# Two of a chunk's four weight sums made by an adding DMA instead of VectorE, in a macaron block with Strassen-Winograd up projections

## The reference

```
def _swiglu(h, w_in, w_out):
    gate, up = jnp.split(h @ w_in, 2, axis=-1)
    return (jax.nn.silu(gate) * up) @ w_out
...
        x = x + FFN_RES * gt1[:, None, :] * _swiglu(h, ffn1_w_in[l], ffn1_w_out[l])
```

## Time and profile before

| | us |
|---|---|
| median of 3 runs | 2106.72 |
| lowest, highest | 2099.39, 2107.37 |
| span of the profiled execution | 2101.5 |

### The profile page before, as it was taken

The page is one execution under the profiler, slowest core; times in us unless marked ns, Lnnn a source line. Parts: engine busy times, 40 slices in busy tenths (PEclk is TensorE's granted clock), DMA queues, the critical chain, the costliest instruction groups (busy, mean ns, idle before and its releaser), DMA issues.

```text
span 2101.5 us, 27713 instructions
## 1 busy us (share of the span) xinstructions
PE 2045.3 (97%) x9921; PEld 1707.3 (81%) x9921; DVE 1370.3 (65%) x1935; ACT 850.6 (40%) x1223; POOL 122.7 (6%) x211
## 2 busy tenths in 40 slices
PE   4999999999999999999999998999999999999998
PEld 4888888888888888888888887887888888888887
DVE  5987777765674567667577578649666666633434
ACT  5432333332343366456456466325333333322322
POOL 6000000001211000000000000000000000001010
PEclk7999999999999999999999999999999999999999
DMA  9344544425865420100111001323233223235453
GB/s 363 98 130 131 142 136 122 120 82 204 301 216 188 130 67 21 40 23 22 32 31 33 19 22 61 100 81 101 80 90 90 70 80 90 85 130 190 163 196 117
DMA packets 185790, 230.87 MB, mean 110 GB/s; under 512 B 7540, under 2 KB 137708, under 8 KB 184940
## 3 DMA queue, kind: packets, MB, share of 16 engines
q1 hardware_dynamic: 155300, 132.72, 20.8%
q0 software_dynamic: 23424, 84.16, 12.0%
q10 hardware_dynamic: 6984, 12.86, 1.8%
HBM read 189.59 MB, written 40.11 MB: 109 GB/s over the span
## 4 chain that ended last, share of the span: by engine, by line
PE 86%; DVE 7%; ACT 3%; DMA 2%; issue 2%; SPq 0%; POOL 0%; DVEq 0%; ACTq 0%
PE ps L728 26%; PE ps L730 25%; PE ps L729 25%; PE ps L997 2%; PE ps L942 1%; PE ps L928 1%; DMA ada_second<-in_w_ada_dram 1%; PE ps L931 1%; PE ps L959 1%; PE ps L958 1%; DMA x_rows<-in_x_dram 1%; PE ps L736 1%; PE ps L744 0%; DMA w_raw<-in_ffn_w_out_dram 0%; PE ps L989 0%
## 5 line engine op out<-in xcount | busy, mean ns | idle before, releaser
L728 PE MATMUL ps<-h_hi,w_hi 128*128 128x512 f32 x720 | 292.9, 407 | 9.1 <-DVE h_lo L1763 5.6
L730 PE MATMUL ps<-h_hi,w_lo 128*128 128x512 f32 x720 | 285.6, 397 | 0.0
L729 PE MATMUL ps<-h_lo,w_hi 128*128 128x512 f32 x720 | 285.1, 396 | 0.0
L728 PE MATMUL ps<-da_hi,dw_hi 128*128 128x512 f32 x704 | 275.6, 391 | 1.3 <-DVE dw_lo L1867 0.9
L730 PE MATMUL ps<-da_hi,dw_lo 128*128 128x512 f32 x704 | 274.1, 389 | 0.0
L729 PE MATMUL ps<-da_lo,dw_hi 128*128 128x512 f32 x704 | 274.0, 389 | 0.0
L728 PE MATMUL ps<-T_hi,op_hi 128*128 128x512 f32 x640 | 249.4, 390 | 0.0
L730 PE MATMUL ps<-T_hi,op_lo 128*128 128x512 f32 x640 | 249.0, 389 | 0.0
L729 PE MATMUL ps<-T_lo,op_hi 128*128 128x512 f32 x640 | 249.0, 389 | 0.0
L1229 ACT ACTIVATE op_hi<-S_f 128x512 fp32r<-128x512 f32 x160 | 100.8, 632 | 309.6 <-PE ps L730 300.4
L1864 DVE TENSOR_TENSOR da_lo<-act_raw,da_hi 128x512 fp32r<-128x512 f32 x88 | 60.9, 692 | 217.9 <-ACT da_hi L1278 217.8
(11 more groups left out here) (286 smaller groups left out, 3513.3 us busy)
## 6 DMA issues: line engine op xcount, KB each, us to landing
w_raw<-in_ffn_w_out_dram POOLq DMA_DIRECT2D x84, 512.0 KB, 3.8
raw<-in_ffn_w_in_dram SPq DMA_DIRECT2D x44, 512.0 KB, 5.3
raw_odd<-in_ffn_w_in_dram SPq DMA_DIRECT2D x44, 512.0 KB, 5.7
act_rows<-act_out SPq DMA_DIRECT2D x44, 512.0 KB, 3.4
act_raw<-act_rows SPq DMA_DIRECT2D x88, 256.0 KB, 2.6
ada_ring<-in_w_ada_dram POOLq DMA_DIRECT2D x32, 512.0 KB, 3.8
raw<-in_w_in_mix_dram SPq DMA_DIRECT2D x29, 512.0 KB, 3.9
ada_late<-in_w_ada_dram POOLq DMA_DIRECT2D x24, 512.0 KB, 4.9
```

Source lines behind the costliest of these rows:

```text
L728: pe.matmul(dst, whi, mhi, start=start, stop=False)
L729: pe.matmul(dst, whi, mlo, start=False, stop=False)
L730: return pe.matmul(dst, wlo, mhi, start=False, stop=stop)
```

## The change

Of the four sums, S0 = a21 + a22 and S2 = a11 + a21 are now made by DMAs. POOL loads one quadrant into the slot from w_in, waits, and adds the other with a DMA whose accumulate operation is an addition. To make both of these additions (S2 was a11 - a21), the lower weight row of the seven products is negated, so the sums S1 and S3, still DVE's, and four reads of products change sign where needed. POOL's new function has two plain DMAs, a wait, and two adding DMAs; for the first Strassen chunk it waits for all T sums, for others until op_lo 6 of the chunk before is written. DVE's `weight_sums` now waits for all four DMAs at its head. POOL's modulation loads of each chunk come behind its sums, and POOL now has an up phase in the second FFN too, between its work for the mixer and the w_out loads. The counter of the silu of c is merged with s_cols.

```diff
-        SUM_AT = {"P5": (0, 1), "P7": (2, 2), "P6": (1, 3), "P3": (3, 4)}
+        SUM_AT = {"P5": (0, 0), "P7": (2, 0), "P6": (1, 1), "P3": (3, 2)}
...
-            def up_body(b, kind, v, k0):
-                if kind & ADDS:
-                    for k in range(k0, k0 + KH):
-                        load_ada(v, k)
-            bodies(pool, ffn1, up_body)
+            def load_sums(f, c):
+
+                if isinstance(c, int) and c == CL:
+                    pool.wait_ge(s_T, (f.i + 1) * T_ALL)
+                else:
+                    pool.wait_ge(s_lo, f.op(c, 6) - Ffn.PRODUCTS)
+                as_k = lambda n: S_f[:, n].rearrange("p (k j) -> p k j", j=P)
+                quad = lambda s, k0: f.w_in[:, k0:k0 + KH, s, c, :]
+                pool.dma_start(as_k(0), quad(1, 0)).then_inc(s_SL, 16)
+                pool.dma_start(as_k(2), quad(0, 0)).then_inc(s_SL, 16)
+                pool.wait_ge(s_SL, f.landed(c, 1))
+                pool.dma_start(as_k(0), quad(1, KH), accum_op=ALU.add).then_inc(s_SL, 16)
+                pool.dma_start(as_k(2), quad(1, 0), accum_op=ALU.add).then_inc(s_SL, 16)
+
+            def up_body(f, b, kind, v, k0):
+                for q in range(2):
+                    if not (kind == LAST and q == 1):
+                        load_sums(f, 2 * b + CL + q + 1)
+                    if kind & ADDS:
+                        for k in range(k0 + 2 * q, k0 + 2 * q + 2):
+                            load_ada(v, k)
+
+            def up(f):
+                load_sums(f, CL)
+                bodies(pool, f, lambda b, kind, v, k0: up_body(f, b, kind, v, k0))
+            up(ffn1)
             ffn_w2(ffn1)
...
+            up(ffn2)
             ffn_w2(ffn2)
...
-                    act.wait_ge(s_S, f.sums(c, SUM_AT[Ffn.ORDER[j]][1]))
+                    made = SUM_AT[Ffn.ORDER[j]][1]
+                    act.wait_ge(*(s_S, f.sums(c, made)) if made else (s_SL, f.landed(c, 2)))
...
                 if isinstance(c, int) and c == CL:
                     dve.wait_ge(s_T, (f.i + 1) * T_ALL)
-                else:
-                    dve.wait_ge(s_lo, f.op(c, 6) - Ffn.PRODUCTS)
...
-                dve.tensor_tensor(S_f[:, 0], a21, a22, ALU.add).then_inc(s_S, 1)
-                dve.tensor_tensor(S_f[:, 2], a11, a21, ALU.subtract).then_inc(s_S, 1)
+                dve.wait_ge(s_SL, f.landed(c, 2))
+                dve.tensor_tensor(S_f[:, 1], S_f[:, 0], a11, ALU.add).then_inc(s_S, 1)
                 dve.wait_ge(s_S, f.sums(c, 1))
-                dve.tensor_tensor(S_f[:, 1], S_f[:, 0], a11, ALU.subtract).then_inc(s_S, 1)
-                dve.wait_ge(s_S, f.sums(c, 3))
-                dve.tensor_tensor(S_f[:, 3], a12, S_f[:, 1], ALU.subtract).then_inc(s_S, 1)
+                dve.tensor_tensor(S_f[:, 3], a12, S_f[:, 1], ALU.add).then_inc(s_S, 1)
...
-                add(u2[:, :], 1, p1_f[:, :])
+                less(u2[:, :], p1_f[:, :], bank(1))
...
-                add(c22[:, :], 3, u3[:, :])
-                add(u4[:, :], 3, u2[:, :])
+                less(c22[:, :], bank(3), u3[:, :])
+                less(u4[:, :], u2[:, :], bank(3))
...
-                add(c21[:, :], 5, u3[:, :])
+                less(c21[:, :], bank(5), u3[:, :])
...
-            act.activation(c_silu[:, :], cols[:, ROW_C:ROW_B], ACT.Silu).then_inc(s_csilu, 1)
+            act.activation(c_silu[:, :], cols[:, ROW_C:ROW_B], ACT.Silu).then_inc(s_cols, 1)
```

More of the change, by code:

```diff
@@ L292, in build @@
         s_hi, s_lo, s_S = sem("ffn_operand_hi"), sem("ffn_operand_lo"), sem("ffn_weight_sums")
+        s_SL = sem("ffn_weight_sums_landed")
         s_prod = sem("ffn_product_done")
@@ L326, in __init__ @@
                 self.silu0 = i * (CL + self.SILUS * n)
-                self.S0 = i * 4 * n
+                self.S0 = i * 2 * n
+                self.SL0 = i * 64 * n
                 self.raw0 = i * 16 * CF
@@ L348, in sums, with landed @@
             def sums(self, c, r):
-                return self.S0 + 4 * (c - CL) + r
+                return self.S0 + 2 * (c - CL) + r
+            def landed(self, c, r):
+                return self.SL0 + 64 * (c - CL) + 32 * r
             def step(self, p, ch):
@@ L1843, in weight_sums @@
                     dve.wait_ge(s_T, (f.i + 1) * T_ALL)
-                else:
-                    dve.wait_ge(s_lo, f.op(c, 6) - Ffn.PRODUCTS)
                 flat = lambda t: t.rearrange("p k j -> p (k j)")
                 R = raw_chunk[q]
-                a11, a12, a21, a22 = flat(R[:, 0, 0:KH]), flat(R[:, 0, KH:KD]), flat(R[:, 1, 0:KH]), flat(R[:, 1, KH:KD])
-                dve.tensor_tensor(S_f[:, 0], a21, a22, ALU.add).then_inc(s_S, 1)
-                dve.tensor_tensor(S_f[:, 2], a11, a21, ALU.subtract).then_inc(s_S, 1)
+                a11, a12 = flat(R[:, 0, 0:KH]), flat(R[:, 0, KH:KD])
+                dve.wait_ge(s_SL, f.landed(c, 2))
+                dve.tensor_tensor(S_f[:, 1], S_f[:, 0], a11, ALU.add).then_inc(s_S, 1)
                 dve.wait_ge(s_S, f.sums(c, 1))
-                dve.tensor_tensor(S_f[:, 1], S_f[:, 0], a11, ALU.subtract).then_inc(s_S, 1)
-                dve.wait_ge(s_S, f.sums(c, 3))
-                dve.tensor_tensor(S_f[:, 3], a12, S_f[:, 1], ALU.subtract).then_inc(s_S, 1)
+                dve.tensor_tensor(S_f[:, 3], a12, S_f[:, 1], ALU.add).then_inc(s_S, 1)
             def operand_lo(f, c, q, j):
@@ L1878, in add, with less @@
                     dve.tensor_tensor(dst, bank(bk), other, ALU.add).then_inc(s_read, 1)
+                def less(dst, a, b):
+                    dve.tensor_tensor(dst, a, b, ALU.subtract).then_inc(s_read, 1)
                 def beside(j):
@@ L2352, in _ @@
             lower_bounds()
-            dve.wait_ge(s_csilu, 1)
+            dve.wait_ge(s_cols, 2)
             for k in range(KD):
```

1 line of the change is left out of this document (removed).

## The result

The change takes 2420.5 us (median of 4 runs, 2415.6 to 2423.1) against 2104.3 for the kernel before: 1.151 times as long, 95% interval 1.148 to 1.154. The prediction was 2420. The profiled span is 2414.0 us against 2101.5, 312.5 us more; the sum of the prediction had 313.4.

What follows compares the result with a forecast made beforehand. PE bounded the kernel before; the DMA loop would set the pace. Heads 11.3 and 12.5, later chunks 161.1 and 125.1, clock 3.4 sum to 313.4 us; with span 2101.5 and 5.2 around it, 2420 us, range 2200 to 2680.

Steps and rivals of the forecast that it cites:

- Part 1: Two DVE instructions fewer per chunk save 0 us, since DVE has idle time there and PE none.
- Part 2: POOL's serial DMA chain closes a loop once per chunk; the chunk takes the larger of 19.05 us and L + W.
- the hiding limit: How much of L DVE's idle time hides: 8.0 us in plain chunks, 5.6 in those with modulation adds.
- W: DVE's work from S1 to the next op_lo 6: 11.0 us, 13.4 with two modulation adds.
- L: Chain from the end of op_lo 6 to the start of S1, two DMA stages: 15.0 us, bounds 9.6 and 23.3.
- Heads: Start of each FFN's Strassen chunks: PE's next chunk starts 11.3 us late in the first FFN, 12.5 in the second.
- Later chunks: 18 more chunk periods per FFN add 161.1 us in the first FFN and 125.1 in the second.
- Clock: PE's clock falls after idle gaps, but only the last chunk of each FFN pays: 2 x 1.7 = 3.4 us.
- lean transfers: Rival: DMAs land faster, L = 7.7 us, plain chunks hide all, 2139 us; chance 0.06.
- Hidden: Rival: chain stays under 5.6 us in every chunk, PE never waits, 2107 us; chance 0.03.
- heavy: Rival: accumulating DMAs cost more, L passes 22 us; 2762 us at L = 24; chance 0.08.
- Cold: Rival: PE stays at the 1.2 GHz level through whole chunks, 17 us over in each of 38, 2757 us; chance 0.03.

Runs made afterwards that it cites:

- e1: The change with a second buffer for S0 and S2, so a chunk's sums load while the chunk before is worked on: 2118.8 us.
- e4: The change with DVE making all four sums again, no sum DMAs on POOL, only the new signs and merged counter kept: 2105.7 us.
- e2: The change with POOL waiting for op_lo 3 of the chunk before instead of op_lo 6: 2237.1 us.
- e6: The change without its second DMA stage, leaving one wait and two plain DMAs in the loop: 2143.9 us.
- e5: The change with one wait added on SP: the next chunk's raw weights load only after the chunk's four sum DMAs have landed: 2337.6 us.
- e3: The change with plain DMAs in place of the adding ones, all waits and sizes kept: 2329.5 us.
- e10: The change with 20 extra matmuls before PE's wait for the first product, in 19 chunks of the second FFN: 2421.6 us, side by side with e9.
- e9: The change itself run once more, on the same chip as e10: 2419.4 us.

## Why the prediction was right, step by step

- Part 1, nothing gained by two DVE instructions less: right. DVE's busy time fell by 69 us (1370.3 to 1301.6; 48 were forecast), the time didn't. e1, with as few instructions, has 1326.1, 44 less. The rest most likely comes with the way busy time is counted: back to back, instructions of 0.68 us start 0.60 apart, and the overlap counts once. e4 and e1 show from both sides that DVE's part is worth nothing.
- Part 2, the loop: right. e1 takes the chain out of the loop and 302 of 316 us are gone; e2 shortens the other arc and the period follows; e6 shows the hiding limit: 8.4 us fit in plain chunks (8.0 by the forecast, 8.5 by the measured W), 8.6 don't in those with adds (5.6 by the forecast).
- L, 15.0 us forecast, 15.7 measured (1.1 too low in the first FFN, 0.3 in the second). Its terms were off by more: the first stage with the wake-up 8.7 us, not 7.4, as it shares the engines with 1.5 MB of other transfers (1 MB of them costs 1.8 to 2.2 us, e5); the second 6.9, not 7.4, in which a plain transfer would be 4.7 and adding costs 2.2 (e3). That an adding DMA costs as much as a plain one was wrong, and was made good by a landing time, 5.7 us, taken from a row twice as large: luck. POOL's 1.08 us per issue, from a slope, was 0.78.
- W, 11.0 and 13.4 forecast, 10.55 and 12.8 measured: the step of 0.617 us was right (sixteen from 2032.89 to 2042.76), and the 0.5 us of allowance for semaphores and dependent pairs, which the step held already, was too much. The two errors, L too low and W too high, nearly cancel in the period: 28.4 forecast and 28.9 measured with adds, 26.0 and 25.8 without.
- Heads: S1 at 93.02 for 93.7, PE's first product at 97.39 for 98.0, op_lo 6 ending at 101.98 for 103.0, the next chunk at 123.70 for 124.5. Counted from the last T sum, PE's second Strassen chunk started 11.2 us late in the first FFN (11.3 forecast) and 12.0 in the second (12.5).
- Later chunks, from the start of P1 in the second Strassen chunk to that in the last: 163.95 us more than before in the first FFN (161.1 forecast) and 122.3 in the second (125.1). The first hides two errors of the forecast. It took the pace before as 19.05 us everywhere, but these 18 chunks took 350.1 us and not 342.9, since in four of them PE also forms a modulation vector (`mod_vector`); in the change that work fits into PE's gaps. And 16 turns had adds, not 15, each 0.5 us longer than forecast. The starts of P1, before (chunk 2, chunk 20), then after (chunk 20; chunk 2 is in the head's lines above):

```profile
113.20 0.39 PE L728 MATMUL ps<-h_hi,op_hi 128*128 128x512 f32 x1
...
463.31 0.39 PE L728 MATMUL ps<-h_hi,op_hi 128*128 128x512 f32 x1
```

```profile
637.76 0.80 PE L754 MATMUL ps<-h_hi,op_hi 128*128 128x512 f32 x1 [4.08 <-DVE u L1904]
```

- The whole: each of these parts is right to 3 us, and their errors nearly cancel. The 5.2 us that the forecast took as lying around the span were mostly the spread between runs: the profiled run of the change took 2415.6 us with a span of 2414.0, and the median of four is 2420.5. The hit to within 1 us is luck; a mechanism that is right to some 10 us is not.
- Clock: right, the loss is real and covered (e10). In the last chunks, which the forecast charged with 1.7 us each, PE took 1.6 us longer than before in the first FFN and 0.1 in the second.
- Rivals: lean transfers needs L = 7.7. Even at the head, beside no load and only a store of 512 KB, the two stages took 11.4 us (81.59, POOL's first issue, to S1 at 93.02). The estimate of 3.2 us per stage from the Trainium skill, page "DMA: Bandwidth & Descriptors", section "Anatomy of one DMA — SWDGE (gpsimd) path", is short of the 4.6 us that the plain stage took there, of which 0.78 are POOL's first issue. That the 512-byte lines are the reason isn't shown. Hidden is refuted by PE's waits, heavy by L = 15.7 us and by e3, in which adding costs 2.2 us and not the 9 that the rival needs. Cold is refuted by the change itself: PE is back at steps of 0.23 us 5 us into the chunk shown, and the granted clock of the plain stretches is 0.89, and e10 shows that the lower level costs nothing here. (Its price adds up to some 2753 us, not 2757.)

## What to carry to other kernels

Before work is moved from an engine that isn't the bound to a DMA, look for the ring: the buffer that must be free, the DMA, the engine that waits at the head of its body, and the last instruction that frees the buffer. Its period is the DMA's latency plus that body, and however idle the engine was, latency beyond its idle time per turn is paid in full, 38 us here for each us. Where the wait starts (183 us for one number in e2) and a second buffer (302 us in e1) brought more here than a faster transfer (91 us in e3), and none of them brought the kernel below its time before.

## What the runs showed of the hardware

- An adding DMA of 256 KB in 512-byte lines holds POOL for 1.29 to 1.82 us against 0.75 to 0.78 for a plain one, and a stage of two takes 6.9 us instead of 4.7 (the change, e3).
- For 512 KB, adding DMAs move 1024 packets of 512 bytes where plain ones of the same lines move 128 of 4096 (896 more per stage in the queue's row, the change against e3).
- A first stage of 0.5 MB took 8.1 us on average beside 1.5 MB of other transfers (the change), 6.2 beside a store of 0.5 MB (e5) and 4.6 at the head.
- Some 4 us of each chunk at the lower clock level cost nothing where PE isn't the bound (e9, e10): the granted clock is then a symptom.
